# Two weight streams and 64 slots for the two smallest of six sorted experts

## What is computed

```python
N_EXPERTS, TOP_K, D_MODEL, D_EXPERT = 8, 2, 1024, 1408

def swiglu(h, w_gate, w_up, w_down):
    return (jax.nn.silu(h @ w_gate) * (h @ w_up)) @ w_down

def moe_ffn(h, w_router, w_e_gate, w_e_up, w_e_down):
    logits = jnp.einsum('bsd,de->bse', h, w_router, preferred_element_type=jnp.float32)
    top_vals, top_idx = lax.top_k(logits, TOP_K)
    top_w = jax.nn.softmax(top_vals, axis=-1)
    combine = jnp.sum(jax.nn.one_hot(top_idx, N_EXPERTS, dtype=jnp.float32) * top_w[..., None], axis=-2)
    y = jnp.zeros_like(h)
    for e in range(N_EXPERTS):
        y = y + combine[..., e:e + 1] * swiglu(h, w_e_gate[e], w_e_up[e], w_e_down[e])
    return y
```

## Time and profile before

| what | value |
|---|---|
| profiled execution, its own time | 1055.26 us |
| its span, first to last instruction | 1053.2 us |
| median of three executions | 1055.7 us |
| PE busy in the span | 1040.3 us, 99% |
| DVE busy | 835.4 us, 79% |
| ACT busy | 678.7 us, 64% |
| POOL busy | 144.8 us, 14% |
| bytes moved | 252.74 MB, mean 240 GB/s |
| the chain that ended last | PE 92%, DVE 5%, ACT 1% |

### The profile page before, as it was taken

The page is one execution under the profiler, slowest core; times in us unless marked ns, Lnnn a source line. Parts: engine busy times, 40 slices in busy tenths (PEclk is TensorE's granted clock), DMA queues, the critical chain, the costliest instruction groups (busy, mean ns, idle before and its releaser), DMA issues.

```text
span 1053.2 us, 15497 instructions
## 1 busy us (share of the span) xinstructions
PE 1040.3 (99%) x5669; PEld 848.2 (81%) x5669; DVE 835.4 (79%) x1164; ACT 678.7 (64%) x971; POOL 144.8 (14%) x177
## 2 busy tenths in 40 slices
PE   8999999999999999999999999999999999999997
PEld 7988888888888888999887878777777777676775
DVE  6879776988666766687967797898898889889885
ACT  7776746556443534676665555877777777777784
POOL 5004332001100000000613000450101010101011
PEclk9999999999999999999999999999999999999999
DMA  9553544567456546363444548799999999999993
GB/s 285 196 163 113 172 128 158 162 230 272 147 209 230 170 140 195 102 221 120 127 164 142 175 143 290 258 388 343 320 357 391 371 333 389 370 388 366 390 378 100
DMA packets 131282, 252.74 MB, mean 240 GB/s; under 512 B 6606, under 2 KB 56868, under 8 KB 131204
## 3 DMA queue, kind: packets, MB, share of 16 engines
q1 hardware_dynamic: 129444, 245.93, 67.0%
q0 software_dynamic: 1296, 4.20, 1.9%
q10 hardware_dynamic: 464, 1.58, 0.4%
HBM read 247.49 MB, written 4.19 MB: 239 GB/s over the span
## 4 chain that ended last, share of the span: by engine, by line
PE 92%; DVE 5%; ACT 1%; issue 1%; DMA 1%; POOL 0%; SPq 0%; DVEq 0%; POOLq 0%; ACTq 0%
PE PS L826 28%; PE PS L1367 12%; PE PS L1369 12%; PE PS L1368 12%; PE PS L1231 8%; PE PS L1232 4%; PE PS L1178 2%; PE PS L1180 2%; PE PS L1179 2%; PE PS L850 2%; DVE m_lo L2223 2%; PE PS L1038 1%; PE PS L1322 1%; DVE scr L2531 1%; DVE big L2523 1%
## 5 line engine op out<-in xcount | busy, mean ns | idle before, releaser
L517 DVE TENSOR_TENSOR w_lo<-ring,w_hi 128x1536 fp32r<-128x1536 f32 (+1 forms) x190 | 304.5, 1618 | 80.0 <-ACT w_hi L504 79.3
L504 ACT ACTIVATE w_hi<-ring 128x1536 fp32r<-128x1536 f32 (+1 forms) x191 | 260.4, 1369 | 99.3 <-PE PS L1232 47.8
L1667 ACT ACTIVATE m_hi<-ring 128x512 fp32r<-128x512 f32 (+2 forms) x256 | 157.8, 632 | 119.7 <-PE PS L826 117.9
L2223 DVE TENSOR_TENSOR m_lo<-ring,m_hi 128x512 fp32r<-128x512 f32 (+2 forms) x256 | 182.3, 743 | 58.3 <-ACT m_hi L1667 56.3
L826 PE MATMUL PS<-m_hi,h_both 128*128 128x512 f32 (+3 forms) x640 | 178.5, 365 | 0.7 <-DVE m_lo L2223 0.6
L826 PEld LDWEIGHTS PS<-m_hi,h_both 128*128 128x128 f32 x640 | 113.0, 188 | 19.9 <-DVE m_lo L2223 2.5
L1231 PE MATMUL PS<-h_both,w_hi 128*128 128x512 f32 x352 | 124.4, 398 | 0.0
L826 PE MATMUL PS<-m_lo,h_both 128*128 128x512 f32 (+3 forms) x320 | 115.0, 359 | 0.0
L1367 PE MATMUL PS<-w_hi,hTe 128*96 128x512 f32 (+1 forms) x288 | 108.8, 378 | 0.0
L1369 PE MATMUL PS<-w_lo,hTe 128*96 128x512 f32 (+1 forms) x288 | 108.1, 375 | 0.0
L1368 PE MATMUL PS<-w_hi,hTe 128*96 128x512 f32 (+1 forms) x288 | 107.7, 374 | 0.0
(11 more groups left out here) (386 smaller groups left out, 1976.1 us busy)
## 6 DMA issues: line engine op xcount, KB each, us to landing
ring<-in_w_in_dram SPq DMA_DIRECT2D x39, 1024.0 KB, 5.2
ring<-in_w_exp_gate_dram SPq DMA_DIRECT2D x48, 768.0 KB, 8.2
ring<-in_w_exp_up_dram SPq DMA_DIRECT2D x48, 768.0 KB, 8.0
ring<-in_w_exp_down_dram SPq DMA_DIRECT2D x24, 1536.0 KB, 8.9
ring<-in_w_branch_dram SPq DMA_DIRECT2D x12, 1024.0 KB, 5.1
ring<-in_w_ffn_gate_dram SPq DMA_DIRECT2D x12, 768.0 KB, 5.5
ring<-in_w_ffn_up_dram SPq DMA_DIRECT2D x12, 768.0 KB, 5.4
ring<-in_w_ffn_down_dram SPq DMA_DIRECT2D x6, 1536.0 KB, 6.3
```

Source lines behind the costliest of these rows:

```text
L504: act.activation(split_parts(u, j)[0], ring[:, i % NSLOT, w0:w0 + words], ACT.Copy)\
L517: dve.tensor_tensor(lo, ring[:, (j // 2) % NSLOT, w0:w0 + words], hi.bitcast(F32), SUB).then_inc(sem(f"lo_ready{b}"), 1)
L1667: act.activation(hi, raw, ACT.Copy).then_inc(sem("m_hi_ready"), 1)
L2223: dve.tensor_tensor(lo, raw, hi.bitcast(F32), SUB).then_inc(sem("m_lo_ready"), 1)
```

## The change

Experts 0 and 1 keep places 0 and 1. The other six are sorted by their number of tokens while place 0 runs: the smallest comes to place 3 and the next to place 6, the rest to 2, 4, 5 and 7 in order of size. What a place was to an expert number before is now looked up: SP reads the expert of each place from 2 on out of a small table, and waits for that table first.

Places 3 and 6 have 64 slots and not 96. Their high and low token parts stand side by side, 64 and 64 columns, as one stationary operand of 128. One matmul with the weights' high part and one with their low part then make all products, token low times weight low among them, but the sums for the low token parts lie in rows 64 to 127. Each group of columns is therefore folded when it is complete: ACT copies the whole bank out of PSUM, and one matmul with a shifted identity adds the copy's lower half to the bank's upper half. There are eight folds in such a place (gate and up of three groups, two halves of the output).

The rest follows from these two. The sort is eight dependent DVE instructions before piece 9 of place 0, and the selection for the six experts moves behind it, to pieces 10 and 11. PE's counts come with the row scales of experts 0 and 1, the scales of the other six after piece 13. POOL's chain for the output rows waits for the sort and has one step more, and the row numbers move from place 0, piece 20, to place 1, piece 3. A gather of three experts is copied in three instructions, as one of them has the other layout. POOL has 40 small memsets more after its last mixer step. The rows of a small place leave 64 at a time, and its output rows are scaled later in the next place (before piece 6). SP's code for the places is written out, not looped.

The core of the diff:

```diff
-CAP = 96
-PASSES = -(-T // CAP)
+CAP, FEW = 96, 64
+SMALL = (3, 6)
+PASSES = -(-T // FEW)
...
-SCALES_AT = 7
-INFO_AFTER = 20
+FEW_AFTER = {2: [("fold", 0)], 4: [("folded", 0)], 5: [("fold", 1)], 7: [("folded", 1), ("gu", 0)], 8: [("fold", 2)],
+             9: [("tr", 0)], 10: [("folded", 2)], 11: [("fold", 3)], 13: [("folded", 3), ("gu", 1)],
+             15: [("tr", 1), ("fold", 4)], 16: [("tr", 2), ("folded", 4)], 17: [("fold", 5)],
+             18: [("folded", 5), ("gu", 2)], 20: [("tr", 3)]}
+FOLDS, DOWN_FOLDS = 8, (6, 7)
+SCALES_AT, SORTED_AT, SCALES_AFTER = 7, 9, 13
+INFO_AFTER = 3
...
+PREVIOUS_FOLDED, PREVIOUS_ROWS, FIRST_ROWS = 2, 6, 8
...
-            with sp.Fori(1, NE) as e:
+            for e in range(1, FIXED):
                 expert_loads(eg, eu, ed, e, e)
+
+            def expert_in(e):
+                return sp.value_load(order[0:1, e:e + 1], min_val=0, max_val=NE - 1)
+
+            sp.wait_ge(sem("routing_known"), ROUTING_KNOWN["order_known"])
+            for e in range(FIXED, NE):
+                expert_loads(eg, eu, ed, expert_in(e), e)
...
+            def folded(r, e, i):
+
+                pe.wait_ge(sem("fold_full"), fold_no(r, e, i) + 1)
+                bank, n = fold_of(i)
+                pe.matmul(PS[:, bank, 0:n], shift[:, :, :], folds[:, i % 2, 0:n], start=False, stop=True,
+                          skip_group_check=True).then_inc(sem("folded"), 1)
...
+                def two(dst, x, whi, wlo, start, stop):
+                    pe.matmul(dst, x, whi, start=start, stop=False)
+                    return pe.matmul(dst, x, wlo, start=False, stop=stop)
...
+                            if e in SMALL:
+                                mm = two(PS[:, 2 * (g % 2) + up, 0:gn * P], hTe_few[:, kt, :, :], hi[:, k, :], lo[:, k, :],
+                                         kt == 0, kt == KD - 1)
+                                continue
...
             free, every_pos = spare[:, 0, :, :], spare[:, 1, :, :]
-            pool.wait_ge(sem("pos_step"), 1)
-            pool.wait_ge(sem("routing_known"), ROUTING_KNOWN["totals_read"])
...
+            pool.wait_ge(sem("routing_known"), ROUTING_KNOWN["order_known"])
...
+                runs = slot_runs(batch)
+                for run in runs:
+                    s0, c0, n = TSLOT[run[0]], (run[0] - e0) * CAP, len(run)
+                    if run[0] in SMALL:
+                        ins = act.activation(few_tokens(run[0])[:, k, 0, :], PS[:, 4 + b, c0:c0 + FEW], ACT.Copy)
...
+            def fold(r, e, n, i):
+
+                bank, words = fold_of(i)
+                x = fold_no(r, e, i)
+                wait_used(act, expert_unit(n), fold_after(i))
...
+                if not isinstance(x, int) or x > 1:
+                    act.wait_ge(sem("folded"), x - 1)
+                act.activation(folds[:, i % 2, 0:words], PS[:, bank, 0:words], ACT.Copy).then_inc(sem("fold_full"), 1)
...
+            def sorted_places():
+
+                dve.wait_ge(sem("totals_full"), 1)
+                dve.wait_ge(sem("constants"), 1 + HALF + 3 + 1)
+                step(dve.tensor_copy(counts, PS[:, LOGIT_BANKS[1], NE:2 * NE]))
+                step(dve.tensor_tensor(key, counts, key_off, ADD))
+                step(dve.tensor_tensor(smaller, key.unsqueeze(1).broadcast_to([P, NE, NE]), key.unsqueeze(2).broadcast_to([P, NE, NE]),
+                                       ALU.is_lt))
+                step(dve.tensor_reduce(size_rank, smaller, AX.X, ADD))
+                step(dve.tensor_tensor(moves, size_rank.unsqueeze(1).broadcast_to([P, NE, NE]),
+                                       rank_at.unsqueeze(2).broadcast_to([P, NE, NE]), ALU.is_equal))
+                step(dve.tensor_tensor(mixed, by_expert.unsqueeze(2).broadcast_to([P, 8, NE, NE]),
+                                       moves.unsqueeze(1).broadcast_to([P, 8, NE, NE]), MUL))
+                step(dve.tensor_reduce(by_place, mixed, AX.X, ADD))
+                dve.tensor_copy(order[:, FIXED:NE], expert_at[:, FIXED:NE]).then_inc(sem("routing_known"), 1)
...
-                for a in range(TT):
-                    selected(a, e0 + ne, NE - ne)
-                dve.wait_ge(sem("psel_ready"), 4 * r + 4)
-                dve.tensor_scalar(pos[:, :, :], pos[:, :, :], float(CAP), None, SUB).then_inc(sem("pos_step"), 1)
-                dve.wait_ge(sem("pos_step"), r + 1)
```

More of the change, by code:

```diff
@@ L86, in expert_after @@
 def expert_after(e, j):
-    what = list(EXPERT_AFTER.get(j, ()))
-    if e == 0 and j == INFO_AFTER:
+    what = list((FEW_AFTER if e in SMALL else EXPERT_AFTER).get(j, ()))
+    if e == 0 and j == SCALES_AFTER:
+        what.append(("scales", 0))
+    if e == 1 and j == INFO_AFTER:
         what.append(("info", 0))
@@ L92, in expert_after, with slot_runs, slots_of, rows_at @@
         what.append(("gather", BATCH_AFTER[j]))
-    return what
+    if e - 1 in SMALL and j == PREVIOUS_FOLDED:
+        what.append(("rows_folded", 0))
+    return what
+def slot_runs(batch):
+    e0, ne = BATCHES[batch]
+    runs = []
+    for e in range(e0, e0 + ne):
+        if e not in SMALL and runs and runs[-1][-1] not in SMALL and TSLOT[e] == TSLOT[runs[-1][-1]] + 1:
+            runs[-1].append(e)
+        else:
+            runs.append([e])
+    return runs
+RANK_AT = [0] + [0] * (NE - 1)
+for _i, _e in enumerate(tuple(range(FIXED)) + SMALL + tuple(e for e in range(FIXED, NE) if e not in SMALL)):
+    RANK_AT[_e] = _i
+def slots_of(e):
+    return FEW if e in SMALL else CAP
+def rows_at(e):
+    return PREVIOUS_ROWS if e in SMALL else FIRST_ROWS if e == 0 else ESPLIT - 1
+def fold_no(r, e, i):
+    return FOLDS * (len(SMALL) * r + SMALL.index(e)) + i
 def place_aux():
@@ L108, in place_aux @@
                     take(("info", 0), 0)
+                elif what == "scales":
+                    take(("scales", 0), 1)
                 elif what == "tr":
@@ L747, in _ @@
                 with sp.Fori(1, npass) as r:
-                    with sp.Fori(0, NE) as e:
-                        expert_loads(eg, eu, ed, e, r * NE + e, again=True)
+                    for e in range(NE):
+                        expert_loads(eg, eu, ed, expert_in(e) if e >= FIXED else e, r * NE + e, again=True)
         @block.tensor
@@ L1358, in row_scales @@
                 mm.then_inc(sem("rsl_full"), 1)
-                if isinstance(r, int):
-                    for a in range(TT):
-                        mm = pe.matmul(totals, ones[:, :], msel[:, a, :], start=(a == 0), stop=(a == TT - 1))
-                    mm.then_inc(sem("totals_full"), 1)
             def expert(r, e, n):
@@ L1428, in expert @@
                         row_scales(r)
+                        if isinstance(r, int):
+                            expert_counts()
                     for what, x in expert_after(e, j):
+                        if what == "folded":
+                            folded(r, e, x)
+                        elif what == "scales":
+                            more_scales(r)
+                        elif what == "rows_folded":
+                            for i in DOWN_FOLDS:
+                                folded(r, e - 1, i)
                         if what == "tr":
@@ L1568, in _ @@
             pool.wait_ge(f, n + 1)
+            for q in range(NE):
+                pool.memset(by_expert[:, 7, q:q + 1], float(q))
+                pool.memset(key_off[:, q:q + 1], q / 16.0 if q >= FIXED else 2.0 * T * (q - FIXED))
+                pool.memset(rank_at[:, q:q + 1], float(RANK_AT[q]))
+                pool.memset(cap_at[:, q:q + 1], float(slots_of(q)))
+                pool.memset(weight_at[:, q:q + 1], CAP / slots_of(q))
             step(pool.memset(tri, 1.0))
@@ L1594, in _ @@
             step(pool.tensor_tensor(pairs, pairs, inv_rms(2 * DEPTH - 1).unsqueeze(1).broadcast_to([P, 2, TT]), MUL))
-            top, second = (m12[:, :, i, :] for i in range(2))
+            top, second = (m12_placed[:, :, i, :] for i in range(2))
             step(pool.tensor_tensor(top, top, rsm[:, 4:6].unsqueeze(2).broadcast_to([P, TT, NE]), MUL))
```

194 lines of the change are left out of this document (144 added, 50 removed).

## The result

| | before | after |
|---|---|---|
| median | 1055.76 us (1055.42 to 1055.93, 8 executions) | 1063.61 us (1059.15 to 1067.25, 8 executions) |
| ratio | | 1.0066, 95% interval 1.0052 to 1.0080 |
| profiled execution, its own time | 1055.26 us | 1060.06 us |
| its span | 1053.2 us | 1058.0 us |
| places 0 to 7, us | 50.2, 51.1, 46.85, 51.15, 46.85, 46.85, 46.85, 47.0 | 53.3, 52.6, 46.85, 53.4, 47.3, 46.85, 42.7, 47.5 |

A forecast was written before the change was run, and what follows sets the result against it. PE was taken to bound the kernel, with other engines and DMA close behind. Terms -3.6 (place 3), -3.3 (place 6) and +2.0 (place 0) sum to -4.9 us: 1055.7 to 1050.8 us, range 1046.0 to 1057.0.

The forecast's parts named there:

- Place 3: Third place of the expert loop: DVE takes over from PE at 47.0 us plus 0.6 waiting, 47.6 us, 3.6 less.
- the split copies: Gathered tokens of place 3 copied in three pieces: up to 2.4 us more on DVE, 2.7 on ACT, lower bound zero.
- Place 6: Second small place: weight loads bound it, 45.0 us at 392 GB/s less a 1.5 us lead, 43.5 us, 3.3 less.
- Place 0: Where the sort is put: DVE 2.7, soon 4.4 us late, partly covered by slack; 2.0 us more, between 0.5 and 3.5.
- the slack taken off: Piece 9 of place 0: PE needs DVE's low part 0.46 us after starting, giving 1.7 us of slack.
- only change place: Counts matmul and row numbers around place 0: they merely move, so no cost was put on them.
- POOL's chain: Output rows in place 0: starts later, may end at 690 to 693; costed at nothing, 2 us kept for the range.
- Places 4 and 7: Places after the small ones: 46.85 us of PE against 45.0 of DMA, so a lost lead does not lengthen them.
- (a): Rival: DMA already full, no place below 46.8 us except by its lead; 1053.2 us in all, chance 0.20.
- (b): Rival: fold handshake makes ACT the bound, 51.5 us in place 3, 46.7 in place 6; 1057.9 to 1060 us, chance 0.12.
- (c): Rival: idle PE gets the lower clock in places 3 and 6, over 1080 us; chance 0.02 together with another rival.
- -4.6 for place 3: Low end of the range: place 3 with no waiting left and half the split cost, part of 1046.0 us.

The follow-up runs named there:

- fill: Changed kernel with matmuls of zeros added into open sums where PE waits in places 3 and 6; 1058.11 us, ratio 1.0023 to the kernel before.
- g4_hold_b: Changed kernel with the second gather moved to place 4 and zero matmuls ahead of waits in places 3 and 6; 1056.16 us, ratio 1.0006 to the kernel before.
- held kernels: Changed kernel with second gather in place 4 and zero matmuls at PE's waits, without and with the sort ahead of the stage; 1056.16 and 1054.67 us.
- small3: Changed kernel with only place 3 small; 1062.71 us, ratio 1.0081 to the kernel before.
- small6: Changed kernel with only place 6 small; 1058.71 us, ratio 1.0028 to the kernel before.
- gather4: Changed kernel with the second gather moved from place 3 to place 4; 1059.89 us, ratio 1.0039 to the kernel before.
- early3_g4_hold_b: Changed kernel with sort ahead of stage, second gather in place 4, more zero matmuls, two put back between ranks and counts; 1053.24 us, 0.9978 of the kernel before.

## Why the prediction was wrong

**Place 3 (47.6 forecast, 53.4 measured): the step that failed.** I took the fullest engine, DVE with 47.0 us, and added 0.6 for waiting. DVE had only 44.7 of work (the split copies came out at my lower bound, zero), ACT 40.9 and not 46.3. But the waiting was nearly 9 us. I carried over as if the waits of a kernel in which PE is late would stay short in one where PE is early. They are short *because* PE is late: DVE's read of the turned rows stands four pieces back in its program, and a PE that runs just behind DVE has to wait those pieces out. With the clock held (`fill`) the place takes 51.8, with 7.2 us in which DVE has nothing to do where I had 0.6; the low clock adds 1.6. With the gather in place 4 and the clock held (`g4_hold_b`) the place takes 44.9, 6.9 us less, of which 4.2 are work that DVE no longer has (40.3 in place of 44.6) and 2.7 are time without work. The 4.6 us without work that are left there go with the loads, which run at 385 GB/s with a share of 1.05.

**Place 6 (43.5 forecast, 42.7 measured): right in mechanism**, in size in part by luck. The loads bound it: its chain runs over two down loads, 8.4 and 10.4 us long. They ran at 384 GB/s instead of the 392 I took, which makes 45.8 us of the 17.6 MB. But the place moved only 42.7 x 384 = 16.4 MB, so it lived on a lead of 3.1 us, twice my 1.5, and the two misses nearly cancel. Place 7 has to make up for it: 13.7 MB, where it had 12.6. I had read the two leads in the earlier trace rows with two landing times, 7.8 us for the first and 9.7 for the second; with 7.8 for both the shorter one is 2.7. In the held kernels place 6 took 1.1 to 2.4 us less than place 3 (43.8 against 44.9, 42.7 against 45.2) at about the same rate. Of the two figures of the Trainium skill (DMA: Bandwidth & Descriptors, Specifications) the 358 GB/s of one core does not hold here; by it place 6 would have gained nothing.

**Place 0 (2.0 forecast, 4.4 measured): mis-sized.** The sort's 2.7 us were right, and so were the 4.4 us of added work on DVE. What was wrong is the slack taken off: PE waits for both parts of a piece before its first matmul, so the 0.46 did not exist; even with the 1.7 us the excess would have grown to 4.4 - 1.7 = 2.7 and not to 2.0; and at the turn at 695.31 nothing of it was left, because "only change place" was wrong for the row scales: after piece 13 they lie in a bank that PE needs for the turn and that DVE reads late in its program. The row numbers did only change place, and I should have put their 1.3 us on place 1. POOL's chain cost nothing, as I had costed it, and ended at 690.4, as I had estimated; its steps took from 0.20 us to the first one's 5.18:

```profile
678.31 5.18 POOL L1713 TENSOR_TENSOR spare<-u,tokf 128x16 f32<-128x16 f32 x1 [24.11 <-DVE order L2965]
683.58 0.20 POOL L1715 TENSOR_SCALAR spare<-u 128x16 f32<-128x16 f32 x1
```

and no wait of PE or DVE for POOL's rows shows. The long step runs beside DVE, which works without a pause from 678.07 to 683.66, mostly on two inputs. That goes in the direction of the lock of the shared ports in the Trainium skill (SBUF — State Buffer, two separate sides), but the page locks for one instruction, and this step lasted as long as five of DVE's; no run here tests the rule.

**Places 4 and 7 (nothing forecast, 0.5 each): missed.** I had the engines pass from a small place to the next at no cost. But the last two of the eight folds, those of the output, stand in the next place's program: two matmuls of 512 columns (L1454, at 870.32 in place 4), 0.46 us by their start-to-start distance, in a place that PE bounds. With one small place only the place behind it pays (`small3`: place 4 47.3, `small6`: place 7 47.5).

**The rivals.** (a), full DMA, is where a cured place 3 ends, but at 45 us and not 46.8: it is the bound that the forecast had for place 6. (b), ACT as the bound through the folds, is refuted: ACT was busy 40.9 us where it needed over 51, and all waits for a fold or by one come to some 3.5 us in the stage. Its time was nearer than mine, for another reason. (c), the lower clock, I gave next to no chance and a price of 25 us or nothing. It happens in between: 3.4 to 6.8 us at a time, in or just behind single gaps. I argued from the earlier trace rows, PE busy 2.1 of 3 us, and from gaps "below a microsecond"; the gaps were up to 4.4 us. It makes the miss larger and is not the cause of it: with the clock mostly held (`fill`) the kernel still takes 1058.1 us, above the 1057.0 that ended my range. One slip changes nothing: the low end's -4.6 for place 3 should be -5.4 by its own terms (-3.6, the waiting 0.6 and half the split cost 1.2).

## What to carry to other kernels

When a change relieves the engine that paced the kernel, don't take the time of the next-fullest engine: list every place where the relieved engine waits for something that stands later in another engine's program, because those waits were hidden only by its lateness, and price each at the distance between the two programs. If two uses share a PSUM bank, check who frees it for whom at the new order of arrival. And when work is added to an engine that runs just ahead of another, don't take the slack of the first step off it: follow the programs to the next place where one waits for the other. Here nearly all the 4.4 us added to DVE came out at such a place.

## What the runs showed of the hardware

TensorE fell to its lower level (clock 0.50, 1.2 GHz) in or just behind gaps of PE: 1.1 us into the 4.39-us gap of place 3, for 6.8 us; at the end of gaps of 2.13 and 2.27 us, for 3.4 us each (`small6`, at 977.6 and 998.1); and even at the end of two waits of 0.88 and 0.57 us with only 16 small matmuls between (place 0 with the early sort, at 671.6). Not every such gap does it: 2.83 and 2.56 us passed at 1.00 in the changed kernel, and 3.01 us (from 987.35) in `gather4`. A handful of zero matmuls ahead of the waits kept place 3 at 1.00, and `fill` lies 5.5 us below the changed kernel with every wait left as it was.

The low stretches make the time of a kernel scatter: over 8 us in the changed one. Where the clocks stay at 0.997 and above, some scatter remains that is not theirs: 2.5 us in `g4_hold_b`, 1.9 us in `early3_g4_hold_b`. The kernel before is not free of them either: two of its executions took 1058.3 and 1059.0 us, at a clock of 0.995. So a single profile may show little of it: the changed kernel's profiled execution was 3.5 us better than its median.
